# A two-layer encoder on one core: low halves of weight tiles moved from GpSimd to VectorE, and the scaling of every second trunk tile from ScalarE to GpSimd

## The reference

```python
hn = rmsnorm(x, norm1_g[l])
q, k, v, hy_in, gates = split(hn @ w_in[l])            # 1024 x 5120
a_out = neighbourhood_attention(rms(q), rms(k), v, rpb)  # 8 heads of 64
b_out = hyena_mixer(short_conv(hy_in), filters)          # long convolution, 512 channels
merged = g[0] * (a_out @ w_up_na[l]) + g[1] * (b_out @ w_up_hy[l])
x = x + merged @ w_out[l]
h = rmsnorm(x, norm2_g[l])
# PEER: product keys pick 16 experts of 16384 for each of 8 heads
q2 = h @ peer_wq[l]; scores, top_k, softmax -> g
a = gelu(h . u_tab[eid]); x = x + sum(g * a * v_tab[eid])
```

## Time and profile before

| | |
|---|---|
| Median of three runs | 1931.53 us (1929.2 to 1931.96) |
| The profiled execution | 1929.89 us, with a span of 1927.8 us |
| Mean granted PE clock | 0.993 of full speed |
| Busy share of the span | PE 97%, ACT 70%, DVE 63%, POOL 54% |
| DMA | 357 MB, 185 GB/s on average |

### The profile page before, as it was taken

How to read it: one execution, slowest core, us unless ns; L and a number is a source line. 1 busy time by engine, 2 the same in 40 slices (tenths; PEclk the granted TensorE clock), 3 DMA queues, 4 the chain that set the end, 5 groups by cost and what they waited for, 6 DMA issues and landing times.

```text
span 1927.8 us, 42946 instructions
## 1 busy us (share of the span) xinstructions
PE 1873.0 (97%) x14238; PEld 1353.3 (70%) x14238; DVE 1218.7 (63%) x2530; ACT 1355.3 (70%) x1929; POOL 1035.3 (54%) x664
## 2 busy tenths in 40 slices
PE   7989999999999999999989899999999989999999
PEld 5777898899998344444457778988999974444444
DVE  5897569777775344444458974796777744444444
ACT  8787988887777455555588879888877765555554
POOL 4655868876667322222256558687776672222221
PEclk8999999999999999999999999999999999999999
DMA  8544656655555566666565446556555555656654
GB/s 265 164 143 142 214 168 201 202 188 173 174 174 167 173 205 203 200 206 200 192 213 167 143 135 227 173 197 201 192 171 167 173 175 175 206 201 202 206 198 140
DMA packets 100324, 357.38 MB, mean 185 GB/s; under 512 B 11744, under 2 KB 13730, under 8 KB 99492
## 3 DMA queue, kind: packets, MB, share of 16 engines
q1 hardware_dynamic: 99828, 354.36, 55.9%
q10 hardware_dynamic: 432, 2.18, 0.3%
HBM read 355.45 MB, written 1.05 MB: 185 GB/s over the span
## 4 chain that ended last, share of the span: by engine, by line
PE 87%; DVE 6%; ACT 5%; issue 2%; DMA 0%; SPq 0%; POOL 0%; DVEq 0%; ACTq 0%; POOLq 0%
PE bank L1992 35%; PE bank L1536 14%; PE bank L1538 14%; PE bank L1540 14%; PE bank L1931 3%; ACT w_hi L504 2%; ACT ring L510 2%; PE bank L1860 1%; DVE arena L1150 1%; DVE arena L1167 1%; PE bank L1911 1%; PE bank L1865 1%; DVE arena L1146 1%; DVE arena L1148 1%; PE bank L1699 0%
## 5 line engine op out<-in xcount | busy, mean ns | idle before, releaser
L462 POOL TENSOR_TENSOR w_lo<-ring,w_hi 128x1024 f16<-128x1024 f32 x404 | 863.9, 2140 | 396.5 <-ACT ring L510 395.9
L504 ACT ACTIVATE w_hi<-ring 128x1024 f16<-128x1024 f32 x654 | 685.0, 1047 | 38.2 <-PE bank L1540 25.2
L1536 PE MATMUL bank<-act_parts,w_hi 128*128 128x256 f16 x2560 | 698.0, 273 | 0.5 <-DVE act_parts L1268 0.5
L1540 PE MATMUL bank<-act_parts,w_lo 128*128 128x256 f16 x2560 | 697.8, 273 | 0.0
L1538 PE MATMUL bank<-act_parts,w_hi 128*128 128x256 f16 x2560 | 697.7, 273 | 0.0
L897 DVE SCALAR_TENSOR_TENSOR w_lo<-ring,w_hi 128x1024 f16<-128x1024 f32 x250 | 306.3, 1225 | 351.7 <-ACT w_hi L504 351.7
L476 POOL TENSOR_TENSOR e_lo<-arena,e_hi 128x256 f16<-128x256 f16 x256 | 171.2, 670 | 480.9 <-ACT e_hi L813 480.9
L510 ACT ACTIVATE ring<-ring 128x1024 f32<-128x1024 f32 x404 | 424.2, 1050 | 0.0
L1992 PE MATMUL bank<-w_hi,e_hi 128*128 128x512 f16 x1024 | 390.3, 381 | 11.3 <-issue 11.3
L1992 PE MATMUL bank<-w_lo,e_hi 128*128 128x512 f16 x1024 | 390.2, 381 | 0.0
L1992 PE MATMUL bank<-w_hi,e_lo 128*128 128x512 f16 x1024 | 389.9, 381 | 0.0
(11 more groups left out here) (258 smaller groups left out, 1862.1 us busy)
## 6 DMA issues: line engine op xcount, KB each, us to landing
ring<-stream SPq DMA_DIRECT2D x654, 512.0 KB, 3.3
arena<-rpb_in SPq DMA_DIRECT2D x8, 512.0 KB, 6.2
arena<-subkeys ACTq DMA_DIRECT2D x2, 1024.0 KB, 5.6
ring<-stream SPq DMA_DIRECT2D x4, 256.0 KB, 4.8
xT<-x_in SPq DMA_DIRECT2D x4, 256.0 KB, 5.2
arena<-w_in SPq DMA_DIRECT2D x2, 512.0 KB
arena<-decay_in SPq DMA_DIRECT2D x2, 512.0 KB
arena<-dft_in SPq DMA_DIRECT2D x2, 512.0 KB, 4.3
```

Source lines behind the costliest of these rows:

```text
L462: pool.tensor_tensor(w_lo[:, slot, :], ring[:, slot, :], w_hi[:, slot, :], ALU.subtract).then_inc(lo_ready.sem, 1)
L504: nc.scalar.activation(w_hi[:, slot, :], ring[:, slot, :], ACT.Copy, scale=TABLE_SCALE).then_inc(hi_ready.sem, 1)
L1536: T.matmul(out_, weights(w_hi, tile, j), hi[:, k, :], start=start, stop=False, skip_group_check=True)
L1540: return T.matmul(out_, weights(w_lo, tile, j), hi[:, k, :], start=False, stop=stop, skip_group_check=True)
```

## The change

There are three edits.

- **Second table.** DVE makes the low halves of all 128 tiles from 200 on. POOL's last low half in a layer is that of tile 199, and ACT no longer scales tiles 200 to 203.
- **Head of a layer.** DVE makes the low halves of tiles 2 to 5 too, so that it has a layer's first six (`VECTOR_HEAD`). In layer 0 those of 2 and 3 stand behind the second and fourth addition of squares, in layer 1 behind the second and fourth pair of low rows; those of 4 and 5 stand behind the sum of squares and ahead of `inverse_rms(1)`. ACT no longer scales these tiles.
- **Odd tiles from 7 to 71.** POOL scales them itself, in place (33 a layer), waits for its own result, and subtracts. ACT still scales the even tiles from 6 to 70 and all of the first table.

`lo_ready` becomes two semaphores, `low_by_vector` and `low_by_pool`; PE and SP wait on the one that belongs to the tile.

```diff
-POOL_TILES = T_VT + RING
+VECTOR_HEAD = 6
+def made_by_vector(tile):
+    return tile < VECTOR_HEAD or tile >= T_VT
+def scaled_by_pool(tile):
+    return VECTOR_HEAD <= tile < T_U and tile % 2 == 1
...
-            def scaled_low(l, i, tile):
+            scaled = [0]
+            def pool_low(l, i, tile):
                 slot = tile % RING
-                pool.wait_ge(ring_scaled.sem, ring_scaled.at(l, i * RING + (tile + 1 - HEAD)))
+                if scaled_by_pool(tile):
+                    pool.wait_ge(hi_ready.sem, hi_ready.at(l, tile + 1))
+                    scaled[0] += 1
+                    pool.tensor_scalar(ring[:, slot, :], ring[:, slot, :], TABLE_SCALE, None, ALU.mult
+                                       ).then_inc(pool_scaled, 1)
+                    pool.wait_ge(pool_scaled, scaled[0])
+                else:
+                    pool.wait_ge(ring_scaled.sem, ring_scaled.at(l, i * RING + scaled_by_scalar(tile)))
                 pool.tensor_tensor(w_lo[:, slot, :], ring[:, slot, :], w_hi[:, slot, :], ALU.subtract
-                                   ).then_inc(lo_ready.sem, 1)
+                                   ).then_inc(low_by_pool.sem, 1)
             def pool_layer(l):
-                pool.wait_ge(lo_ready.sem, lo_ready.at(l, HEAD))
-                for tile in range(HEAD, RING):
-                    scaled_low(l, 0, tile)
-                with pool.Fori(1, POOL_TILES // RING) as i:
+                for tile in range(VECTOR_HEAD, T_U):
+                    pool_low(l, 0, tile)
+                with pool.Fori(0, NK // RING) as i:
                     for s in range(RING):
-                        scaled_low(l, i, s)
+                        pool_low(l, i, T_U + s)
...
             def scale_tile(tile):
                 slot = tile % RING
-                nc.scalar.activation(ring[:, slot, :], ring[:, slot, :], ACT.Copy, scale=TABLE_SCALE
-                                     ).then_inc(ring_scaled.sem, 1)
+                if not made_by_vector(tile) and not scaled_by_pool(tile):
+                    nc.scalar.activation(ring[:, slot, :], ring[:, slot, :], ACT.Copy, scale=TABLE_SCALE
+                                         ).then_inc(ring_scaled.sem, 1)
...
                         raw_low_pair(b)
                         if not l:
                             head_low(b % 2, b // 2)
+                        elif b % 2:
+                            low_part(l, 0, HEAD + b // 2)
                 for b in range(KT // 2):
                     add_squares(b, pair_sum, bank[6 + b % 2][:, :])
+                    if not l and b % 2:
+                        low_part(l, 0, HEAD + b // 2)
...
+                for tile in range(RING, VECTOR_HEAD):
+                    low_part(l, 0, tile)
                 inverse_rms(1)
...
                 burst(TGROUPS // RING - 1, False)
+                low_part(l, 0, T_VT)
                 store_late(0, LATE - 3)
-                dve.wait_ge(lo_ready.sem, lo_ready.at(l, POOL_TILES))
+                low_part(l, 0, T_VT + 1)
                 for n in range(LATE - EDGE, LATE):
                     store_late(0, n, last_fresh)
-                with dve.Fori(0, (TILES - POOL_TILES) // RING) as i:
+                    low_part(l, 0, T_VT + RING + n - LATE)
+                with dve.Fori(1, NK // RING) as i:
                     for s in range(RING):
-                        low_part(l, i, POOL_TILES + s)
+                        low_part(l, i, T_VT + s)
```

More of the change, by code:

```diff
@@ L89, with lows_by_engine, scaled_by_scalar @@
 PI_BELOW = 3.1415925
+def made_by_vector(tile):
+    return tile < VECTOR_HEAD or tile >= T_VT
+def scaled_by_pool(tile):
+    return VECTOR_HEAD <= tile < T_U and tile % 2 == 1
+def lows_by_engine(tile):
+    return sum(made_by_vector(t) == made_by_vector(tile) for t in range(tile + 1))
+def scaled_by_scalar(tile):
+    return sum(not made_by_vector(t) and not scaled_by_pool(t) for t in range(tile + 1))
 class Signal:
@@ L272, in encoder_kernel @@
         hi_ready = sig("hi_ready", TILES)
-        ring_scaled = sig("ring_scaled", POOL_TILES - HEAD)
-        lo_ready = sig("lo_ready", TILES)
+        ring_scaled = sig("ring_scaled", scaled_by_scalar(TILES - 1))
+        low_by_vector = sig("low_by_vector", lows_by_engine(TILES - 1))
+        low_by_pool = sig("low_by_pool", lows_by_engine(T_VT - 1))
+        pool_scaled = sem("pool_scaled")
         tile_done = sig("tile_done", TILES)
@@ L358, in encoder_kernel, with low_wait @@
         block = ctx.enter_context(nc.Block())
+        def low_wait(eng, l, i, tile):
+            made = low_by_vector if made_by_vector(tile) else low_by_pool
+            eng.wait_ge(made.sem, made.at(l, i * RING + lows_by_engine(tile)))
         @block.sync
@@ L365, in load, with refill @@
                              ).then_inc(ring_full[slot].sem, 16)
-            def refill(turn, slot):
-                sp.wait_ge(lo_ready.sem, turn * RING + (slot + 1 - RING))
-                load(turn * RING + slot, slot)
+            def refill(l, i, group, slot):
+                tile = (group - 1) * RING + slot
+                if group:
+                    low_wait(sp, l, i, tile)
+                else:
+                    low_wait(sp, l - 1, i, TILES + tile)
+                load(i * RING + (l * TILES + group * RING + slot), slot)
             def layer_loads(l):
@@ L400, in layer_loads @@
                 for slot in range(RING):
-                    refill(l * GROUPS + 1, slot)
+                    refill(l, 0, 1, slot)
                     taps(slot)
                 for slot in range(RING):
-                    refill(l * GROUPS + 2, slot)
+                    refill(l, 0, 2, slot)
                     if slot == 0:
@@ L410, in layer_loads @@
                     for slot in (2 * (r % 2), 2 * (r % 2) + 1):
-                        refill(l * GROUPS + 3 + r // 2, slot)
+                        refill(l, 0, 3 + r // 2, slot)
                         if slot % 2 == 0:
                             offsets(r)
-                with sp.Fori(l * GROUPS + 5, (l + 1) * GROUPS) as turn:
+                with sp.Fori(0, T_VT // RING + 1 - 5) as i:
                     for slot in range(RING):
-                        refill(turn, slot)
+                        refill(l, i, 5, slot)
+                with sp.Fori(0, GROUPS - 1 - T_VT // RING) as i:
+                    for slot in range(RING):
+                        refill(l, i, T_VT // RING + 1, slot)
             def load_x(b):
@@ L442, in _ @@
                     for slot in range(RING):
-                        refill((l + 1) * GROUPS, slot)
+                        refill(l + 1, 0, 0, slot)
             def store(n, b, tokens):
@@ L786, in act_layer @@
                     norm_high(2, (s,))
[L787 to L790, removed]
+                for tile in range(T_WQ + 3 * RING, T_U + RING):
+                    high_part(l, 0, tile)
+                    scale_tile(tile)
                 for n in range(8):
@@ L836, in act_layer @@
                     late_gelu(0, n)
-                with act.Fori(0, TGROUPS // RING) as i:
+                with act.Fori(0, TGROUPS // RING - 1) as i:
                     for s in range(RING):
                         late_gelu(i, EDGE + s)
+                for n in range(LATE - EDGE - RING, LATE - EDGE):
+                    late_gelu(0, n)
                 for n in range(LATE - EDGE, LATE):
@@ L897, in low_part @@
                 V.scalar_tensor_tensor(w_lo[:, slot, :], ring[:, slot, :], TABLE_SCALE, w_hi[:, slot, :],
-                                       ALU.mult, ALU.subtract).then_inc(lo_ready.sem, 1)
+                                       ALU.mult, ALU.subtract).then_inc(low_by_vector.sem, 1)
             def head_low(tile, half):
@@ L908, in head_low @@
                                        w_hi[:, tile, columns], ALU.mult, ALU.subtract
-                                       ).then_inc(lo_ready.sem if half else head_lo[tile], 1)
+                                       ).then_inc(low_by_vector.sem if half else head_lo[tile], 1)
             def dve_layer(l):
@@ L1525, in parts_ready @@
                 def parts_ready(i, tile):
-                    pe.wait_ge(lo_ready.sem, lo_ready.at(l, i * RING + (tile + 1)))
+                    low_wait(pe, l, i, tile)
                 def weights(part_, tile, k):
@@ L2001, in v_last @@
                 pe.wait_ge(e_lo_ready.sem, e_lo_ready.at(l, n + 1))
-                pe.wait_ge(lo_ready.sem, lo_ready.at(l, T_VT + n + 1))
+                low_wait(pe, l, 0, T_VT + n)
                 ins = v_half(n, half, False, n == NK - 1)
```

5 lines of the change are left out of this document (1 added, 4 removed).

## The result

The changed kernel takes 1964.99 us (median of 4 runs, 1963.55 to 1966.0), the kernel before 1931.35 us in the same measurement. The ratio is 1.0176, 95% interval [1.0158, 1.0193]: 34 us slower. Forecast were 1915 us and a range up to 1938.

The account below looks back on a forecast made before the run. PE bounds the kernel (87% of the last-ending chain), so only its idle or slow time pays. Switch -16.6, heads -10.3, attention +9.7 and -2.0, Hyena +2.8, queries 0: -16.4, so 1915 us; range 1901 to 1938, forecast's own 1908 to 1922.

Parts of the forecast that it names:

- half the slope: POOL's new scaling: half the two-input cost per column plus 0.18 us fixed, so 1.16 us for 1024 columns.
- the upper bound of 2.14 us: POOL's new scaling: at most as slow as its two-input subtraction of 1024 columns; the lower bound was 1.05 us.
- just covered, cost 0: Queries: six pairs behind tile 60 lose 1.3 us, hidden by its low half being made 1.96 us early.
- the 0.6 us that DVE was to lose for each us of POOL: Attention stage: DVE's loss to POOL's 14 scalings of 1.16 us, 9.7 us in all, reaching PE.
- The rival (a): POOL's scaling is as slow as its subtraction, 2.14 us: +14.9 us, 1946 us, slower; chance 0.16.
- Switch, forecast -16.6: Second-table start, two layers: PE's 5.7 us waits vanish (11.3 us), and the low-clock tails behind them (5.3 us).
- Heads, forecast -10.3: Layer heads: shorter waits for low halves, value product and L872/L569 give 8.0 us, low-clock tails 2.3 us.
- Tile 7 comes some 0.5 us late: Layer head: tile 7's low half delays PE some 0.5 us, but PE waits for the values behind it anyway.
- The rule: Queries: POOL's time per pair of tiles beyond PE's 5.24 us accumulates, less tile 48's low half being 4.05 us early.
- the 1.28 at which the cost was to begin: Queries: POOL's scaling costs PE time only from 1.28 us upward; 1.16 us was expected.
- Mixers, forecast +10.5 (9.7 - 2.0 + 2.8): Attention: DVE's loss to POOL 9.7, one ACT scaling less before the first exponential -2.0; Hyena: DVE collisions 2.8 us.
- about 17: Attention stage: PE's wait before the transposed probabilities grows from 9.4 to about 17 us.

Follow-up runs that it names:

- edit 1: Table switch alone, on the kernel before: DVE makes the low halves of tiles 200 to 203 too; 1914.79 us, ratio 0.9922.
- where the scaling took 1.11 us: Changed kernel with POOL's scaling cut to 352 of 1024 columns, the rest of those tiles left unscaled; 1905.29 us, ratio 0.9869.
- edits 1 and 2: Changed kernel without POOL's scaling (ACT scales those tiles), so only the second-table and layer-head edits; 1909.95 us, ratio 0.9896.
- the two extra-operation kernels: edits 1 and 2 plus one POOL operation before each odd mixer tile's low half: one-input multiplication 1921.09 us, repeated two-input subtraction 1963.27 us.
- the one-input extra: edits 1 and 2 plus a POOL multiplication by 1.0 on 768 columns before each odd mixer tile's low half; 1921.09 us, ratio 0.9957.
- the two-input scaling: Changed kernel with POOL's scaling written as a product of the slot and a broadcast constant column; 1970.27 us, ratio 1.0208.

## Why the prediction was wrong

The step that failed is a size: "With one input instead of two I take half the slope, 0.18 + 0.98 = 1.16 us", and with it the upper bound of 2.14 us "as slow as with two inputs". Measured were 2.80 us. The trace had no one-input operation of this engine at this shape, and that two inputs cost more than one was assumed, not read. With the price failed the step that hung on it, "just covered, cost 0" in the queries: they cost 37.3 us. A second step failed by itself, the 0.6 us that DVE was to lose for each us of POOL. The rival (a) had the direction and the mechanism in the queries, and put its price at that upper bound. The stated range ended at a scaling of about 1.85 us; already (a) at 2.14 us, 1946 us, lay outside it. With 2.80 us the prediction's own terms give -16.6 - 10.3 + 28.3 + 36.5 = +37.9 us, close to the +35.8 of the profiled execution; that is in part luck, for the heads won 4.6 us less than their term and the mixers lost 7.3 us less than theirs. Term by term:

- **Switch, forecast -16.6: measured -16.8** for both layers, in every kernel with edit 1. The wait of 5.7 us and the tail at half the clock both go, as worked out from the earlier trace rows.
- **Heads, forecast -10.3: measured -5.7**, and -11.7 where the scaling took 1.11 us. The value product's two waits were forecast near 2.4 and 1.1 us, 3.5 together. In the changed kernel they are no longer there: the 3.8 us at L1747 are waits for POOL's low half of tile 11. At 1.11 us they are 1.7 us each, 3.4 together. That the sum agrees is partly luck: edits 1 and 2 had lengthened the wait of layer 1 from 3.1 to 4.4 us, and the shorter chain of ACT then gave 2.7 us in each layer where 2.0 were forecast. "Tile 7 comes some 0.5 us late" rested on the price: PE waits 2.3 us for it at 2.80 us (L1584), and 0.6 at 1.11.
- **Queries, forecast 0: measured +37.3.** The rule was right. It says 12 pairs a layer at 7.15 - 5.24 = 1.91 us less the head start of 4.05, 18.9 us; 18.6 and 18.7 were measured. With 1.11 us, a little below the 1.28 at which the cost was to begin, 1.7 us a layer were lost: the forecast's limit was slightly too high.
- **Mixers, forecast +10.5 (9.7 - 2.0 + 2.8): measured +21.0.** Three errors, not all in one direction. The price was 2.4 times too low. The share of 0.6 of POOL's time that DVE loses, read from collisions with two-input subtractions, was carried over to a one-input operation that DVE shares for most of its length. At 2.80 us and 0.6 the same terms give (14 x 0.6 x 2.80) + 6.8 - 2.0 = 28.3 us, more than the 21.0 measured, and at 1.11 us the mixers lost nothing (-0.5) where the forecast had 10.5. The measured share was 0.25. And the sum had no term for the clock in the mixers, where half of the 21.0 us is PE's work at the 1.2 GHz level. That the probabilities' wait came out at the 16.7 us that I had forecast as "about 17" is the first two errors in one number, not a confirmation.

The Trainium skill (GPSIMD Engine Reference, Engine selection) calls one-input work roughly line-rate. The trace contradicts it for the scaling: 2.77 to 3.02 us for 1024 columns against the 1.03 us that the prediction had worked out from it; the f32 to f16 cast, at 1.04 us, fits.

The Trainium skill (SBUF — State Buffer, Who interferes with whom) says that a DVE instruction with two inputs in this memory contends with a GpSimd instruction that reads it. The trace agrees for the subtraction (2.32 us for 0.48) and, for the scaling, in about its first microsecond only: DVE's 0.48 us at 96.17 lies inside one. That page's rule by itself doesn't tell the two extra-operation kernels apart, and they differ by 42 us.

What stays open: why the multiplication is slow inside the engine, and why it lets DVE through after its first microsecond (reading first and writing later would look like this; no run here shows the phases). How the mixers' loss divides between DVE held by the scaling itself and subtractions that now come in pairs was not measured apart: the 12.6 us of the one-input extra have both. Nor is it shown why the two-input scaling costs so much more in the mixers than the longer one: over both layers it makes DVE busy only 5.5 us longer (32.1 against 26.6 over edits 1 and 2), while PE idles 15.5 us longer. Which of DVE's operations is held seems to matter there, and no run separates that.

## What to carry to other kernels

Price an operation that the trace doesn't show by a run of it, or by a bound that doesn't assume fewer inputs to be cheaper; a handful of forms fit into one run. Before an engine takes over work from another, write its period beside the consumer's: here 7.15 against 5.24 us, which settles the queries by itself. What an engine does to its neighbour depends on the form as well as on the length: judge a replacement by both, for the shorter form here was the dearer one in the stage that DVE paces.

## What the runs showed of the hardware

- On GpSimd, for 128 x 1024 elements of f32: multiplication by an immediate 2.77 to 2.80 us, multiplication by a broadcast column 1.93, multiplication of two tensors 2.40 (one instruction), copy 1.38 and cast to f16 1.04 (one each). Subtraction of an f16 tensor from an f32 one into f16 took 2.14. The first took 1.09 us for 352 columns and 2.13 for 768.
- A DVE operation of the convolutions, 0.48 us with both inputs in SBUF, took 2.0 to 2.4 us when it began in the first 0.3 us of a two-input operation of GpSimd, and 0.48 us inside the later part of a multiplication by an immediate. DVE's L998, which has one of its two tensor inputs in PSUM, took 0.48 to 0.49 us in all its 32 instances, beside both kinds of GpSimd work.
- In the mixers DVE lost 0.63 us for each us of two-input work added on GpSimd, and 0.21 to 0.25 us for each us of one-input multiplication.
- 42 operations of 2.2 us on GpSimd cost 53 us of kernel time in one form and 11 in the other.
